# A router product on the raw residual rows, with the root and the shift applied to its logits, and fused residual steps

## The reference

```python
x_lat = x_lat + gt1 * rmsnorm(y_lat, norm_post_mix[l])
h_lat = modulate(rmsnorm(x_lat, norm_pre_ffn[l]), sh2, sc2)     # h * (1 + scale) + shift
f_lat = expert_choice_ffn(h_lat, w_router[l], w_gate[l], w_up[l], w_down[l])
x_lat = x_lat + gt2 * rmsnorm(f_lat, norm_post_ffn[l])
...
aff = jax.nn.softmax(jnp.einsum("btd,de->bte", h, w_router).astype(jnp.float32), axis=-1)
top_aff, top_idx = lax.top_k(jnp.swapaxes(aff, 1, 2), cap)      # 16 experts, 32 tokens each
xin = jax.vmap(lambda hb, ib: hb[ib])(h, top_idx)
g, u = xin @ w_gate[e], xin @ w_up[e]                           # 1024 x 1024 per expert, in short
y = (silu(g) * u) @ w_down[e] * top_aff                         # and y is added back at the tokens
```

## Time and profile before

| | us |
|---|---|
| median of 3 runs | 1094.0 |
| lowest, highest | 1091.75, 1095.06 |
| the profiled execution | 1093.72 |
| its span, first to last instruction | 1091.9 |
| PE busy | 919.3 (84%) |
| DVE busy | 335.6 (31%) |
| ACT busy | 205.4 (19%) |
| POOL busy | 49.7 (5%) |
| bytes moved | 310.2 MB, mean 284 GB/s |

### The profile page before, as it was taken

How to read it: one execution, slowest core, us unless ns; L and a number is a source line. 1 busy time by engine, 2 the same in 40 slices (tenths; PEclk the granted TensorE clock), 3 DMA queues, 4 the chain that set the end, 5 groups by cost and what they waited for, 6 DMA issues and landing times.

```text
span 1091.9 us, 11355 instructions
## 1 busy us (share of the span) xinstructions
PE 919.3 (84%) x4456; PEld 475.2 (44%) x4456; DVE 335.6 (31%) x605; ACT 205.4 (19%) x441; POOL 49.7 (5%) x113
## 2 busy tenths in 40 slices
PE   3999999999899789667776676666767989999997
PEld 2666564764644522222222222222223775644773
DVE  2199615472561431111111111011013364512022
ACT  2123321221452310000000000000004113411121
POOL 0200000000201000000000000000001000000000
PEclk9799999999999899998888888888889998999999
DMA  9963632642798979999999999999999297004200
GB/s 347 344 248 126 221 132 100 231 154 77 272 338 346 345 287 429 427 429 428 430 427 429 429 429 429 429 428 429 427 428 369 97 343 268 0 20 155 77 1 38
DMA packets 65623, 310.20 MB, mean 284 GB/s; under 512 B 2753, under 2 KB 4980, under 8 KB 52916
## 3 DMA queue, kind: packets, MB, share of 16 engines
q1 hardware_dynamic: 63124, 301.04, 69.0%
q0 software_dynamic: 2464, 8.68, 2.4%
HBM read 308.66 MB, written 1.05 MB: 284 GB/s over the span
## 4 chain that ended last, share of the span: by engine, by line
PE 56%; DMA 33%; DVE 5%; ACT 2%; issue 2%; SPq 1%; POOL 0%; POOLq 0%; ACTq 0%; DVEq 0%
PE bank L846 32%; DMA ring<-w_up_dram 27%; PE bank L1228 8%; PE bank L865 3%; PE bank L1511 3%; DMA ring<-w_ada_dram 2%; DMA ring<-w_in_dram 2%; DMA ring<-w_down_dram 2%; PE bank L1418 1%; PE bank L993 1%; DVE ilat L2400 1%; PE bank L1248 1%; PE bank L876 1%; PE bank L1424 1%; PE bank L855 1%
## 5 line engine op out<-in xcount | busy, mean ns | idle before, releaser
L1228 PE MATMUL bank<-ring,ilat 128*32 128x512 f32 x984 | 147.1, 749 | 104.2 <-DMA ring<-w_up_dram 103.2
L1228 PEld LDWEIGHTS bank<-ring,ilat 128*32 128x32 f32 x984 | 40.4, 133 | 206.8 <-issue 205.7
L2353 DVE TENSOR_TENSOR state<-state,bank 64x512 f32<-64x512 f32 x16 | 11.0, 690 | 302.8 <-ACT state L1765 302.8
L846 PE MATMUL bank<-ring,hT 128*128 128x512 f32 x224 | 97.1, 593 | 0.0
L846 PE MATMUL bank<-hT,ring 128*128 128x256 f32 (+1 forms) x320 | 90.4, 445 | 4.0 <-DVE hT L1959 2.0
L846 PE MATMUL bank<-ring,kT 128*128 128x512 f32 (+1 forms) x192 | 82.2, 584 | 3.4 <-ACT kT L1541 2.6
L846 PEld LDWEIGHTS bank<-hT,ring 128*128 128x128 f32 x320 | 64.2, 203 | 29.4 <-issue 19.4
L1248 PE MATMUL bank<-ring,ilat 128*32 128x512 f32 x512 | 58.9, 596 | 14.7 <-ACT ilat L1769 12.7
L846 PEld LDWEIGHTS bank<-ring,hT 128*128 128x128 f32 x224 | 42.4, 190 | 52.6 <-issue 51.7
L1261 PE MATMUL bank<-state,ilat 128*128 128x512 f32 x128 | 59.2, 605 | 0.9 <-DVE state L2357 0.9
L1765 ACT ACTIVATE state<-bank 64x512 f32<-64x512 f32 x16 | 9.5, 591 | 251.6 <-PE bank L1228 251.6
(11 more groups left out here) (354 smaller groups left out, 1042.4 us busy)
## 6 DMA issues: line engine op xcount, KB each, us to landing
ring<-w_down_dram SPq DMA_DIRECT2D x32, 2048.0 KB, 23.6
ring<-w_up_dram SPq DMA_DIRECT2D x31, 2048.0 KB, 23.3
ring<-w_gate_dram SPq DMA_DIRECT2D x30, 2048.0 KB, 18.8
ring<-w_ada_dram SPq DMA_DIRECT2D x24, 2048.0 KB, 9.1
ring<-w_in_dram SPq DMA_DIRECT2D x8, 2048.0 KB, 12.4
ring<-fno_w_in_dram SPq DMA_DIRECT2D x4, 2048.0 KB, 12.9
ring<-w_out_dram SPq DMA_DIRECT2D x2, 2048.0 KB, 8.4
ring<-mla_w_in_dram SPq DMA_DIRECT2D x2, 2048.0 KB, 18.2
```

The lines of the kernel that those rows point to most:

```text
L846: ins = pe.matmul(o, l, r, start=start and i == 0, stop=stop and i == len(terms) - 1)
L1228: ins = pe.matmul(bank[0][32 * t:32 * t + 32, :], xin_cur[:, j, :], x[:, n0:n0 + TN], start=j == 0, stop=j == J - 1)
L2353: dve.tensor_tensor(hm, eg, bank[0][64:P, :], ALU.mult).then_inc(freed[0], 1)
```

## The change

**Router and gather.** `normalise` before the router is gone. PE transposes the raw `xr3`, ACT takes one half of a block and DVE the other, unmodulated. The router's weights are scaled by (1 + scale) beforehand, and the sum of shift * router over the model dimension goes through one small product to give a constant per expert; DVE forms logit * root + constant for each block. The one-hot rows of the gather carry the root (`row_pick`), formed by DVE for expert 0 and by POOL for the others. So tmpb (`xn`) and the first gate row G[0] are free once y is added.

**Residual steps of y and f.** `add_normed` makes y * gate while the root is still being formed, and then one fused operation per half: xr = (y * gate) * root + xr. DVE waits for ACT's square of a bank before it reads it.

**Transfers.** Two more extra places (half of pair as tmpb, and G[0]), slot 2 one turn ahead too, and the first two rows j of expert 2's slots 0 and 1 are loaded as soon as gate_up(0) has used them (`second_rows`).

**Order.** The latent of block 1 is made after the router product in two halves, so its tiles of w_down are issued then. The scatter goes by blocks. After the experts, values and key copies move between engines, both blocks of x2T are turned ahead of `pa`, and the second and fourth late product move behind the cqT/ckT copies and behind the rope.

The core of the diff:

```diff
-            slot_uses[s] += E - 1 if s < 2 else E
+            slot_uses[s] += E - 1 if s < 3 else E
...
-        extra = [(0, 0, JH, gates[:, 0:JH * D]), (1, 0, 2, vda[:, :]), (1, 2, JH, kT[:, :]), (2, 0, 2, ctxb)]
-        ahead = [1, 1, 0, 0, 0, 0]
+        extra = [(0, 0, JH, gates[:, 0:JH * D]), (1, 0, 2, vda[:, :]), (1, 2, JH, kT[:, :]), (2, 0, 2, ctxb),
+                 (2, 2, JH, tmpb), (3, 0, 1, G[0])]
+        ahead = [1, 1, 1, 0, 0, 0]
...
+            def second_rows(j):
+                sp.wait_ge(sem("first_rows"), j + 1)
+                for s in range(2):
+                    w, half = expert_tiles[s]
+                    sp.dma_start(expert_slot(s)[:, j * D:(j + 1) * D], expert_src(w, 2, half)[:, j * D:(j + 1) * D])\
+                      .then_inc(sem("second_rows"), 16)
...
             with pool.Fori(1, E) as e:
                 pool.wait_ge(sem("gathered"), e)
-                pool.wait_ge(sem("turned"), e)
+                pool.tensor_tensor(row_pick, onehot2[:, :, bass.ds(e * CAP, CAP)],
+                                   rr[:, 4:4 + TB].rearrange("p (b c) -> p b c", c=1).broadcast_to([P, TB, CAP]),
+                                   ALU.mult).then_inc(sem("row_pick"), 1)
...
-            for b in range(TB):
-                pe.wait_ge(sem("x1_normed"), b + 1)
+            def residual_turned(b):
                 for g in range(2):
-                    turn_chunks(("x1T", b, g), xn[:, b, :], g, True)
-                if b == 0:
-                    for i in range(TB):
-                        context_latent(i)
...
+                    wait_copied(pe, ("y", b, g))
+                    turn_chunks(("x1T", b, g), xr3[:, b, :], g, True)
+
+            residual_turned(0)
+            context_latent(0)
+            residual_turned(1)
+            mod_gate(LATER_GATES[0])
...
             for b in range(TB):
                 branch_norm("y", b)
                 residual_norm(0, b)
-            turned_modulated(("x1T",), h2T, FFN, bs=[0])
+                o = wait_filled(act, ("x1T", b, 0))
+                frees(st, act.activation(h2T[:, 0:4, b * P:(b + 1) * P],
+                                         o[:, :].rearrange("p (j t) -> p j t", j=4), ACT.Copy), ("x1T", b, 0))
...
+            def add_normed(tag, i, b, between=None):
+
+                for n in range(2):
+                    o = wait_filled(dve, (tag, b, n))
+                    cs = slice(n * TN, (n + 1) * TN)
+                    if n:
+                        dve.wait_ge(sem("mean_square"), branch_root[tag, b])
+                    else:
+                        dve.wait_ge(sem("branch_squared"), 2 * i + b + 1)
+                    step(dve.tensor_tensor(xn[:, b, cs], o[:, :], G[i][:, cs], ALU.mult))
+                if between:
+                    between()
+                st.settle()
+                dve.wait_ge(sem("rstd_y"), 2 * i + b + 1)
+                for n in range(2):
+                    cs = slice(n * TN, (n + 1) * TN)
+                    frees(st, dve.scalar_tensor_tensor(xr3[:, b, cs], xn[:, b, cs], rr[:, b:b + 1], xr3[:, b, cs],
+                                                       ALU.mult, ALU.add), (tag, b, n))
...
+            add_normed("y", 0, 0)
+            o = wait_filled(dve, ("shift_logits",))
+            frees(st, dve.tensor_copy(shift_logits, o[:, 0:E]), ("shift_logits",))
+            add_normed("y", 0, 1, lambda: take_turned(0))
+            take_turned(1)
...
+                ins = dve.scalar_tensor_tensor(logit[:, b, :], o[:, b * E:(b + 1) * E], rr[:, 4 + b:5 + b], shift_logits,
+                                               ALU.mult, ALU.add)
...
-            for b in range(TB):
-                add_branch("f", 1, b, TB + b + 1)
-            for b in range(TB):
-                normalise(1, b, "x2_normed")
+            for b in range(TB):
+                add_normed("f", 1, b)
+            normalise(1, 0, "x2_normed")
+            take_keys(2)
+            normalise(1, 1, "x2_normed")
```

More of the change, by code:

```diff
@@ L1754, in _ @@
                                          .broadcast_to([P, 2, ROPE]), ACT.Copy), ("kvc", b))
-            for b in range(TB):
-                act.wait_ge(sem("logit_max"), b + 1)
-                frees(st, act.activation(aff[:, b, :], bank[turns[("logit", b)][0]][:, 0:E], ACT.Exp,
-                                         bias=mx[:, b:b + 1], accum_out=rs[:, b:b + 1]), ("logit", b))
             o = wait_filled(act, ("kvcT",))
@@ L2278, in normalise @@
                 step(dve.tensor_scalar(xn[:, b, :], xr3[:, b, :], rr[:, 4 + b:5 + b], None, ALU.mult), signal)
[L2280 to L2283 removed]
+            over_experts = lambda x: x.rearrange("p (j e) -> p j e", e=1).broadcast_to([P, J, 32])
+            dve.wait_ge(sem("router_in"), 32)
+            step(dve.tensor_tensor(router_shift, router, over_experts(mc[:, FFN, 0, :]), ALU.mult))
@@ L2369, in _, with take_keys @@
             down_out(E - 1)
-            for m in range(2):
+            def take_keys(m):
                 o = wait_filled(dve, ("knc", m))
```

195 lines of the change are left out of this document (119 added, 76 removed).

## The result

The changed kernel takes 1077.98 us (median of 4 runs, 1076.77 to 1078.89) beside 1094.53 for the kernel before (4 runs, 1091.75 to 1096.92). The ratio is 0.9844, with a 95% interval of 0.9825 to 0.9863. Two repeats of both kernels side by side gave 0.9867 (0.9844 to 0.9890) and 0.9849 (0.9828 to 0.9870). The forecast was 1081.0, between 1075 and 1089.

The account below looks back on a forecast made before the run. The expert weights' stream, 428 GB/s from 395 us on, was taken to bound the kernel. Gains of 6.6 + 3.5 + 2.6 = 12.7 us from the profiled 1093.72 gave 1081.0 us, range 1075 to 1089.

Parts of the forecast that it names:

- term 1: Ahead of the experts: idle time of the weight stream falls from 12.1 to 5.5 us, 6.6 us less.
- slack of 2.4 us: At expert 3's first tile: issued at 429.5, full rate 431.3, backlog until 433.7, so the stream's lead survives narrowly.
- I charge a queued piece nothing: In the stream ahead of the experts: five more DMAs, four of 0.5 MiB, cost no extra time when queued.
- rival D: In the stream: each small piece pays its own start, five at 1.8 us, 9 us in all, giving 1090; 5%.
- the second gap: Ahead of expert 0's w_down tiles: the stream idles 2.85 us before their transfer starts at 378.55.
- Term 2: From the last scatter's start to the end of pa: 25.7 us instead of 29.2, 3.5 us less.
- Term 3: MLA entry: PE's waits ahead of qr and kn go, 3.5 us, less 0.9 for a values product: 2.6 us.
- A: Whole kernel: the forecast's own case, with a time of 1078 to 1086; 60%.
- B: Ahead of the experts: the stream's gain is larger, up to 10.3 us, giving 1077; 12%.
- C: Part given back: expert 3's slack overdrawn or new PE waits; 6.7 us gained, giving 1087; 15%.
- The hole that I named as proof against me: In the expert stream: a hole between 395 and 440 us would show the forecast wrong.
- F: TensorE's lower clock from 386 to 430 us delays expert 3's tiles, up to 32 us lost, about 1105; 4%.

Follow-up runs that it names:

- more_quarters: Changed kernel with rows 2 and 3 of expert 2's first tiles issued as four 0.5 MiB DMAs instead of two of 1 MiB; 0.9 us slower by the medians.
- gates_later: Changed kernel with ACT's squares before its copy, kvc(1) before the affinities' transposes, and the last two gate products behind kvc's transposes; 0.9850 (0.9826 to 0.9875).
- again_b: A repeat of the changed kernel with no edit; the two repeats measured 0.9867 and 0.9849 of the kernel before.
- scatter_old: Changed kernel with scatter products in the old order, by column half, then block, both banks awaited first; by its ratio not to be told from the changed kernel.

## Why the prediction held, and where it was off

The direction and the place were right; 1077.98 lies 3.0 us under 1081.0. Against the kernel before beside it the three sets of runs gained 16.5, 14.5 and 16.1 us. What the traces show of the change adds up to 5.6 + 0.9 + 4.7 + 3.1 = 14.3 us where I had 12.7: term 1 was over-estimated, terms 2 and 3 under-estimated, and that these errors partly cancel is luck. By its own steps:

**What bounds the kernel** held: 428 GB/s from 395 us on in both, and of the 6.0 us that the stream had gained by 400 us 5.6 came out at the last w_up tile. Most of the rest went near 430 us: expert 3's first tile was issued at 431.25, not 429.5, and 430 to 440 us brought 415 GB/s, so the slack of 2.4 us was about used up.

**Term 1, 6.6 us.** The landing came 3.8 us sooner. Without the trail, which was 1.26 in the kernel before and 3.08 in this execution, it is 458.4 - 452.8 = 5.6. So the mechanism was right and the term mis-sized. Of the 2.8 us that it lacked, 1.8 is the trail, which no row could have told. The other 1.0 is a balance. The step that failed is "I charge a queued piece nothing", with the pieces that "queue behind them without a gap": from 386 to 400 us the stream lost 2.2 us, 1.4 of it in packets of the four quarters. That is no price of a small piece as such, as more_quarters and gates_later show; it fits pieces issued into a thin queue. It is far below rival D's 9 us, and below the estimate of 10 by the Trainium skill's "DMA: Bandwidth & Descriptors", whose 2.0 us are fitted to DMAs that GpSimd issues, and these are SP's: there are no starts to be seen, since they overlap. Against it, about 1.2 us less was lost ahead of 386 us than I had counted: kvc(1) was done sooner (w_down at 373.97, not 376.8), and the second gap was 1.3 us and not 2.85. The first rows came at 386.97 and not 387.5, though the gather ran at 1.2 GHz.

**Term 2, 3.5 us**, gave 4.69, and 0.94 more in a place that I had not counted. Two steps failed. The 0.94 is the scatter's: I took over its start, 827.05, and overlooked that its first product now waits for one bank instead of two. Of the 1.19 by which 4.69 exceeds 3.5, 0.8 is a term counted twice: my 6.5 us for a block of pa are half of a stretch that had block 1's transposes inside, while I also put these transposes ahead of pa; pa took 12.19 us, not 13.0. The rest is pa's start, at +12.18 and not +12.7. The block order is 1.7 us in all; the fused addition, on which I rested most, 1.1. The remaining 2.8 or so (4.69 + 0.94 less these two) lie in the order of roots, keys and values and in turning both blocks ahead of pa, which I did not take apart.

**Term 3, 2.6 us**, gave 3.13. Undone, the late order costs 2.9. PE does not wait for late_mod: the pair at 894.64 and the columns after it run on. The 1.42 us behind it is no term of mine and most likely not the change's: the repeat again_b has 53.61 us there with the same code, as the kernel before has 53.36.

**The rivals.** A came nearest, though the time lies just under its 1078. B is near the measured time, but for another reason: the gain over my sum is in term 2, not in the stream. C did not happen in the three profiled executions of the changed kernel, and yet it was the nearest danger. The hole that I named as proof against me, between 395 and 440 us, appeared in four of my own variants, in which PE waited 2.82 to 6.10 us for expert 1's w_up: 356 to 410 GB/s over 420 to 430 us. In all four the first piece stood 34.0 us or more behind y(1, 0)'s tile, and one of them, scatter_old, has the changed kernel's stream code. F in small is its mechanism: the lower clock in half a gate_up, some 1.8 us, and then a late slot. I had put F's price at up to 32 us and decisive from 15 on; what it took in these variants was 0.5 to 2. My argument against it, that PE is busier in the new entry, did not hold: over 386 to 392 us the clock was 0.72 where it had been 1.00.

## What to carry to other kernels

When one stream bounds a kernel, count what is in the queue at the moment that each slot comes free; a piece may be small if that closes a hole (here the early quarters left 2.2 us lost where the old order lost 4.6), and it cost least where most was still queued ahead of it. Cut it along the free dimension and keep all 128 partitions. Compare the median of the packets as well as the mean before you put a price on a size. Judge such changes by the landing of the last tile less the engines' trail, since this stayed within 0.5 us in five executions of the same stream code, where the time of one kernel moves by 3 to 6. scatter_old, with that code too, shows that it can still move by 2 when a hole opens. And look at what stands behind a wait on TensorE: a product at half clock can free the next slot late.

## What the runs showed of the hardware

- The sixteen DMA engines of one saturated queue drift apart and stay so: late in the experts the last one's landing stands 1.1 to 3.1 us behind the mean, differently in each execution of the same code, and it had stood there for over 300 us. That is up to 2 us of spread in the time.
- DMAs into partitions 0 to 63 or 64 to 127 moved 225 GB/s, with all engines busy; into 128 partitions 428.
- Packets of 16 KB took 611 ns, of 8 KB 309, of 4 KB 159 (medians). In the changed kernel's first pieces a quarter of the 4 KB packets took longer, and the mean was 199 to 207; further back in the queue they moved 418 GB/s.
- In gate_up(1) TensorE went to 1.2 GHz with waits of 2.82 to 6.10 us for w_up (five executions) and stayed at 2.4 GHz with 0.51 to 1.80 us (nine). Behind the same last wait of 6.15 us the way to the scatter took 11.6 us in four executions (the kernel before's without its 0.91 us wait ahead of the scatter) and 14.1 to 14.5 in seven. What decides between these is open.
